# Inverse roots of the latent, query, key and neighbourhood-key norms moved from GpSimd's power to ScalarE's square root and VectorE's reciprocal

## The reference

```python
h = rms_norm(x, g_mix_norm); proj = h @ w_in
q  = (rms_norm(c_q, g_q_a) @ w_q_b).reshape(B, S, 8, 96)
kv = (rms_norm(c_kv, g_kv_a) @ w_kv_b).reshape(B, S, 8, 128)
q_nope = rms_norm(q_nope, g_q[:64]) * scale
q_pe = rope(rms_norm(q_pe, g_q[64:])) * scale
k_nope = rms_norm(k_nope, g_k[:64])
k_pe = rope(rms_norm(k_pe, g_k[64:]))
# dense attention of q on k; then 2-D neighbourhood attention:
q = rms_norm(na_q, g_q) * dh ** -0.5; k = rms_norm(na_k, g_k)
# rms_norm(x, g) = x * rsqrt(mean(x * x) + EPS) * g
x = x + concat(rms_norm(o_A), rms_norm(o_B)) @ w_out
x = x + hier_moe(rms_norm(x))          # top 1 group, top 2 of its 4 experts
```

## Time and profile before

| | us |
|---|---|
| median of 3 runs | 536.64 |
| the three runs | 536.80, 536.64, 532.17 |
| span of the profiled execution | 534.7 |
| TensorE busy in it | 479.6 (90%) |
| GpSimd busy | 171.8 (32%) |
| VectorE busy | 218.4 (41%) |
| ScalarE busy | 146.0 (27%) |
| mean granted TensorE clock | 0.947 of full |

### The profile page before, as it was taken

One profiled execution on the slowest core, in us unless ns is written; L12 is line 12 of the kernel. 1 busy time (PEld: TensorE's weight loads), 2 busy tenths in 40 slices (PEclk: granted clock), 3 DMA queues, 4 the chain that ended last, 5 costly groups with the idle time before them and its releaser, 6 DMA issues. The chain is left out here.

```text
span 534.7 us, 7730 instructions
## 1 busy us (share of the span) xinstructions
PE 479.6 (90%) x2848; PEld 233.6 (44%) x2848; DVE 218.4 (41%) x688; ACT 146.0 (27%) x332; POOL 171.8 (32%) x175
## 2 busy tenths in 40 slices
PE   4899699998999999999999998619999999999970
PEld 3454454544455556555556555514333333333220
DVE  1125454412375555554555838606322222233110
ACT  2200150404455456553443433300000001100010
POOL 1302078878049980000000202210064222222422
PEclk9999799999699999999999989758999999999995
DMA  7999800000600000058000248983989999999512
GB/s 290 428 371 405 318 0 2 1 0 8 248 1 1 1 0 2 1 218 332 0 2 2 58 179 327 371 317 92 353 309 391 394 373 366 377 386 386 127 15 34
DMA packets 29609, 100.05 MB, mean 187 GB/s; under 512 B 5376, under 2 KB 6912, under 8 KB 29184
## 3 DMA queue, kind: packets, MB, share of 16 engines
q1 hardware_dynamic: 21216, 84.04, 40.4%
q0 software_dynamic: 5904, 8.43, 6.7%
q10 hardware_dynamic: 2448, 7.04, 3.5%
HBM read 77.39 MB, written 35.21 MB: 211 GB/s over the span
## 5 line engine op out<-in xcount | busy, mean ns | idle before, releaser
L1296 PE MATMUL bank<-arena 128*128 128x512 f32 (+1 forms) x256 | 112.7, 589 | 5.2 <-DVE arena L877 3.1
L1605 PE MATMUL bank<-arena 128*32 128x512 f32 x832 | 95.5, 600 | 0.1
L599 POOL DMA_INDIRECT out<-arena x25 | 38.7, 1549 | 128.4 <-issue 72.3
L1296 PEld LDWEIGHTS bank<-arena 128*128 128x128 f32 x256 | 48.5, 197 | 53.9 <-issue 47.7
L1271 PEld LDWEIGHTS bank<-arena 128*128 128x128 f32 (+1 forms) x380 | 46.8, 144 | 47.2 <-issue 41.5
L1271 PE MATMUL bank<-arena 128*128 128x128 f32 (+1 forms) x380 | 56.4, 283 | 11.4 <-DMA arena<-in_x 4.7
L1451 PE MATMUL bank<-arena 128*128 128x512 f32 x112 | 55.5, 619 | 0.5 <-issue 0.5
L1605 PEld LDWEIGHTS bank<-arena 128*32 128x32 f32 x832 | 26.3, 111 | 60.0 <-issue 60.0
L1625 PE MATMUL bank<-arena 128*32 128x512 f32 x416 | 48.4, 593 | 0.9 <-DVE arena L1215 0.8
L953 DVE COPY arena<-bank 128x512 f32<-128x512 f32 (+2 forms) x64 | 35.8, 581 | 23.0 <-PE bank L1271 22.9
L833 ACT ACTIVATE arena<-bank 128x256 f32<-128x256 f32 x13 | 5.0, 384 | 136.3 <-PE bank L1605 136.3
(11 more groups left out here) (162 smaller groups left out, 511.4 us busy)
## 6 DMA issues: line engine op xcount, KB each, us to landing
arena<-in_w_gu SPq DMA_DIRECT2D x17, 2048.0 KB, 14.5
arena<-in_w_dn SPq DMA_DIRECT2D x17, 1024.0 KB
slot_rows<-arena SPq DMA_DIRECT2D x1, 11308.0 KB, 38.0
arena<-slot_rows ACTq DMA_DIRECT2D x13, 514.0 KB
arena<-in_w_out SPq DMA_DIRECT2D x2, 2048.0 KB, 8.2
arena<-in_x SPq DMA_DIRECT2D x4, 512.0 KB, 10.7
arena<-in_w_in_k SPq DMA_DIRECT2D x1, 2048.0 KB, 16.0
arena<-in_w_in_q SPq DMA_DIRECT2D x1, 2048.0 KB, 22.0
```

The source lines that it names most:

```text
L599: nc.gpsimd.indirect_dma_start(out=out_rows, out_offset=bass.IndirectOffsetOnAxis(ap=tag_row[:, g, run:run + 1], axis=0), in_=y_sb[g % 3], ...
L1296: last = nc.tensor.matmul(product_bank(i)[:, 0:width], hT[:, k, t * P:(t + 1) * P], w[:, k, :], start=(k == 0), stop=(k == KD - 1))
L1605: last = nc.tensor.matmul(GU[g % 2][BLK * b:BLK * (b + 1), :], xT[g % 2][:, k, BLK * b:BLK * (b + 1)], w_gu[n % RING][:, k, :], start=(k = ...
```

## The change

Six of the seven power instructions on GpSimd are taken out: latent, four of queries and keys, neighbourhood keys. In place of each ScalarE takes the square root of the variance (`deviation`), and VectorE takes the reciprocal of that. The seventh, for neighbourhood queries, stays on GpSimd, as do the roots of x, of the attention outputs and of x1. The semaphore `s_sqrt` ("deviation_ready") goes from ScalarE to VectorE, and `s_nakr` from VectorE to GpSimd for the neighbourhood keys.

```diff
-                inverse_root(("qk", t), flat(rs_qk[:, t]), 3 * H)
             rotate_q(T - 1)
             for w, (name, buf) in enumerate((("nak", nak), ("naq", naq))):
                 for t in range(T):
                     square(3 * T + w * T + t, sq_qk[t % 2][:, 0:NAW], buf[:, t, :], mme_after(product[name, t]))
-                inverse_root((name, 0), flat(rs_na[:, w]), T * H)
+                if w:
+                    pool.wait_ge(s_var, dve_roots.index((name, 0)) + 1)
...
+                if w:
+                    pool.wait_ge(s_root, root["naq", 0] + 1)
+                else:
+                    pool.wait_ge(s_nakr, 1)
...
+            def deviation(key, v):
+                act.wait_ge(s_var, dve_roots.index(key) + 1)
+                nc.scalar.activation(v, v, ACT.Sqrt).then_inc(s_sqrt, 1)
...
             for t in range(T):
                 projection("lat", t, lat, LAT)
+            deviation(("lat", 0), flat(rs_lat))
             for t in range(2):
                 projection("nak", t, nak, NAW)
             for t in range(T):
                 queries_keys(t)
+                if t > 0:
+                    deviation(("qk", t - 1), flat(rs_qk[:, t - 1]))
             for t in range(2, T):
                 projection("nak", t, nak, NAW)
+            deviation(("qk", T - 1), flat(rs_qk[:, T - 1]))
             qk_turned(0)
...
             qk_turned(2)
+            deviation(("nak", 0), flat(rs_na[:, 0]))
             projection("naq", 3, naq, NAW)
             qk_turned(3)
...
-            dve.wait_ge(s_root, root["lat", 0] + 1)
+            dve.wait_ge(s_sqrt, dve_roots.index(("lat", 0)) + 1)
+            link(nc.vector.reciprocal(rs_lat, rs_lat))
...
             def qk_norm(t):
-                dve.wait_ge(s_root, root["qk", t] + 1)
+                dve.wait_ge(s_sqrt, dve_roots.index(("qk", t)) + 1)
+                link(nc.vector.reciprocal(rs_qk[:, t], rs_qk[:, t]))
...
             for t in range(T):
                 na_means(0, t)
+            nak_scales()
```

More of the change, by code:

```diff
@@ L225, in build @@
         s_x1sq, s_h2s, s_lg, s_lgr = sem("x1_squared"), sem("h2_ready"), sem("logits_ready"), sem("logits_read")
-        s_var, s_root = sem("variance_ready"), sem("root_ready")
+        s_var, s_sqrt, s_root = sem("variance_ready"), sem("deviation_ready"), sem("root_ready")
+        s_nakr = sem("nak_scales_ready")
         s_k, s_zeros, s_zero = sem("constants_in"), sem("zeros_ready"), sem("slots_zeroed")
@@ L273, in bank_read @@
             return (s_tpa if act else s_tpe)[p % 2], sum(same)
-        roots = [("x", t) for t in range(T)] + [("lat", 0)] + [("qk", t) for t in range(T)] + [("nak", 0), ("naq", 0)]
+        roots = [("x", t) for t in range(T)] + [("naq", 0)]
         roots += [("oa", t) for t in range(T)] + [(w, t) for t in range(T) for w in ("ob", "x1")]
@@ L465, in link @@
                 pool.wait_ge(c_pool, n[0])
-            def inverse_root(key, v, n):
-                pool.wait_ge(s_var, dve_roots.index(key) + 1)
-                nc.gpsimd.tensor_tensor(v, v, mhalf[:, 0:n], ALU.pow).then_inc(s_root, 1)
             def inverse_root_of(ms, rs):
@@ L490, in square @@
                 nc.gpsimd.tensor_tensor(dst, src, src, ALU.mult).then_inc(s_sqr, 1)
-            def flat(v):
-                return v.rearrange("p a b -> p (a b)")
             def rotate_q(t):
@@ L502, in _ @@
                 square(t, sq[t % 2][:, 0:LAT], lat[:, t, :], mme_after(product["lat", t]))
-            inverse_root(("lat", 0), flat(rs_lat), 3 * T)
             pool.wait_ge(s_rope, 32)
@@ L515, in _ @@
                     square(3 * T + w * T + t, sq_qk[t % 2][:, 0:NAW], buf[:, t, :], mme_after(product[name, t]))
-                inverse_root((name, 0), flat(rs_na[:, w]), T * H)
+                if w:
+                    pool.wait_ge(s_var, dve_roots.index((name, 0)) + 1)
+                    nc.gpsimd.tensor_tensor(rs_na[:, w].rearrange("p a b -> p (a b)"), rs_na[:, w].rearrange("p a b -> p (a b)"),
+                                            mhalf[:, 0:T * H], ALU.pow).then_inc(s_root, 1)
             pool.wait_ge(s_rb, 16 * H)
@@ L542, in _ @@
             for w, (name, buf) in enumerate((("nak", nak), ("naq", naq))):
-                pool.wait_ge(s_root, root[name, 0] + 1)
+                if w:
+                    pool.wait_ge(s_root, root["naq", 0] + 1)
+                else:
+                    pool.wait_ge(s_nakr, 1)
                 for t in range(T):
@@ L673, in queries_keys, with flat @@
                                    src[:, :, NOPE:]).then_inc(s_mme, 1)
+            def flat(v):
+                return v.rearrange("p a b -> p (a b)")
+            def deviation(key, v):
+                act.wait_ge(s_var, dve_roots.index(key) + 1)
+                nc.scalar.activation(v, v, ACT.Sqrt).then_inc(s_sqrt, 1)
             def qk_turned(t):
@@ L917, in na_means, with nak_scales @@
                     nc.vector.tensor_scalar(rs_na[:, w], ms_na[:, w], 1.0 / DH, EPS, ALU.mult, ALU.add).then_inc(s_var, 1)
+            def nak_scales():
+                dve.wait_ge(s_sqrt, dve_roots.index(("nak", 0)) + 1)
+                nc.vector.reciprocal(rs_na[:, 0], rs_na[:, 0]).then_inc(s_nakr, 1)
             def qk_means(t):
```

## The result

| | before | changed |
|---|---|---|
| runs | 4 | 4 |
| median, us | 536.21 (532.17 to 536.80) | 527.26 (526.54 to 528.47) |
| ratio | | 0.9857 [0.9812, 0.9902] |
| span of the profiled execution | 534.7 | 526.6 |
| mean granted clock | 0.947 | 0.957 |

The change makes the kernel 1.4% faster, where 0.5% was predicted, and 527.26 lies under the range's lower end. On another chip the same change gave 0.9895 [0.984, 0.995]: about 5 us, not 9.

A forecast was written before the change was run, and what follows sets the result against it. TensorE, 90% busy, was taken to bound the kernel, with one wait due to a power, at the latents. Terms -1.8 - 1.1 + 0.25 = -2.65 us took 536.64 to 534.0 us; range 529.5 to 537.7.

The forecast's parts named there:

- the chain of 2.41 us: From the latents' variance to VectorE's scaling: 0.6 us in place of 2.41, so 1.8 us gained.
- the pause: TensorE's wait for VectorE to read the first turned latents: from 4.26 us to about 2.5.
- the table loads: ScalarE's loads before the latents' root and the exponentials: both covered, cost nothing; a rival of 6% had them uncovered, 537.7.
- the margin of tile 3's root: Before tile 0's turning: tile 3's variance ready at 90 to 90.5, over 1 us before ScalarE comes at 91.6.
- ScalarE's queue: Square root before tile 0's turned keys and queries: 0.25 us lost; as a rival, TensorE held up, 6%.
- the clock in the pause: Clock still falls around TensorE's wait but is low for less of the first projections: 1.1 us back, ends 0 and 2.8.
- The clock at the scores: At the scores' start the clock was taken to fall; the rival, 12%, had it stay up: up to 5 us, 529.5.
- GpSimd's powers: Seven powers, 29.8 us on GpSimd: worth nothing by themselves, only where TensorE waits for something they hold up.
- root and queue: Latents' root 1.8 us gained, less 0.25 us for the square root in ScalarE's queue before tile 0's turning: 1.55.

The follow-up runs named there:

- rest_only: Changed kernel with the latents' root again a power on GpSimd, the other five roots on ScalarE and VectorE: 528.80 us, ratio 0.9962.
- delay9: Changed kernel with nine small VectorE operations behind the latents' reciprocal, 1.8 us later: 530.13 us, ratio 0.9997.
- before_more12: Kernel before with twelve more one-column memsets on GpSimd ahead of the attention outputs' roots: 531.02 us, ratio 0.9996.
- filled: TensorE's first group of neighbourhood value projections moved from behind the first scores to ahead of them; on the changed kernel 527.36 us, ratio 0.9885.
- the latents' half: Changed kernel with only the latents' root on ScalarE and VectorE, the other roots again powers on GpSimd: 530.16 us, ratio 0.9924.
- the change again: Changed kernel as it is, run again beside the kernel before: 527.92 us, ratio 0.9895.
- before, filled: Kernel before, powers kept, with the first neighbourhood value projections moved ahead of the first scores: 532.27 us, ratio 0.9997.
- the four kernels made later: Kernel before with 3, 7 or 11 small VectorE operations before the latents' scaling, changed kernel with 5 behind the reciprocal: 534.79, 531.34, 532.45, 527.04 us.

## Why the prediction was wrong

**Right, to a few tenths:** the chain of 2.41 us, 0.55 now (predicted 0.6); the pause (1.8 less); the table loads, both covered, 0.85 and 0.8 us ahead of their activations; the margin of tile 3's root (0.64 us, "over 1"). ScalarE's queue cost 0.10 us, not 0.25: I counted the whole instruction, and the next starts 0.11 behind it. The term's lower end of 0.20 was too high too, though in rest_only the same stage is 0.47 us longer. By these steps and the clock's 1.15 us the profiled execution would have gained 2.9 us, 2.65 predicted.

**Right in the number, and in part by luck:** the clock in the pause, 0.48 + 0.67 = 1.15 us back (1.1 predicted, for a low clock that the shorter pause makes shorter). It was low for 3.4 us in place of 6.8, but it is 3.4 us too in rest_only, delay9 and before_more12, whose pause is 5.1 us. Turning and first projections up to nak 2 take 20.9 us before, 19.7 changed, and 19.4, 19.2 and 19.4 in these three. So the kernel before was compared in an execution where the low clock was long; that the shorter pause made it shorter is not shown.

**The step that failed is the sum's silent term that the rest stays as it was**: from the scores to the end it put the gain at nothing, and it took 536.64 as the time from which to subtract. In the profiled execution that rest gained 5.0 us (3.89 - 0.41 + 1.56). Three things are in it.

*The clock at the scores.* I held a fall there for the rule and a clock that stays up for a rival of 12%. It stayed up, and so it did in nearly all the profiles taken since. Of the 19 profiles taken after the one before, one has the fall, and it is one of the changed kernel with six more memsets (0.76 over 131 to 151 us, 23.75 us for the 100 matmuls, in place of 19.86), with the same idle rows of 0.54 and 0.97 us before it as the others that are not filled. So the stretch of waits allows the fall and doesn't decide it. One in 19 makes the fall look too rare for the kernel before: the two profiles that have it are those with the lowest mean clock (0.947 and 0.949; the others have 0.952 to 0.966), and of its 93 runs 38 are at 0.950 or less, against 3 of 17 of the changed kernel. By that, as an estimate, the fall comes in four of ten executions before and in fewer now; that all these runs have it at the scores is not shown. The rival's place was right, its price (up to 5 us) nearly, 3.9; its chance was not.

*One profile and three runs stood for the kernel before.* Over 93 runs in the five sessions it takes 528.1 to 538.3 us, median 532.6: 530.4 where its mean clock is about 0.96 (12 runs), 537.1 where it is about 0.943 (16 runs). At a clock of 0.952 or less were 52 of these 93, and 3 of 17 of the changed kernel. The profiled execution (0.947) and the median of 536.64 are of the slower half. I had seen the one run in three that was 4.5 us faster, and used it for a rival only; it said that the sum was made against one of several levels. Of the 9 us measured at first, some 4 are this choice of runs: the other comparisons give 5.

*The end as TensorE's.* The prediction took the experts to follow TensorE, and put "GpSimd's powers" at "nothing by themselves". There the last to end is GpSimd's chain, which can swallow part of what TensorE gains (in the latents' half the last output comes 10.8 us earlier than before and the end 6.0, with a last lag of 11.4 in place of 6.9), and its start moved with the count of instructions. And the powers of queries and keys were worth about 2 us at the same clock (rest_only 2.1, delay9 2.2, ± 0.7 each), with TensorE's pause as before.

What the gain of about 5 us consists of: 2.7 to 3.6 us at the same clock (the change again, and with six memsets; ± 1.0), where root and queue were to give 1.55; and 0.006 and 0.003 more of mean clock in the same two sets (0.955 against 0.950, 0.956 against 0.953 beside them), 2.3 and 1.1 us by the slope, where 1.1 was predicted. The unfilled halves add up to it (1.3 and 2.1 at the same clock). **Open** stays in what way the roots of queries and keys give their part. GpSimd's gap is the candidate, and its price is resolved only as 1.1 ± 0.8; "rest only" gives 2.1 ± 0.7 unfilled and, filled, no more than "before, filled", though that one has the gap and it has not. Open too is why low clocks are rarer in the changed kernel at places far behind the pause. That they are rarer is shown by the runs (3 of 17 against 52 of 93); that the shorter pause does it is not, for rest_only, with the pause of before, has a mean clock of 0.959 beside 0.955, and the four kernels made later show only that time and lateness don't go in step.

## What to carry to other kernels

Look for the work that ends last in every stage, above all the last one: a chain of DMAs that each wait for the one before may end a kernel in which TensorE is busy nine tenths of the time, and it gives back or swallows what is gained ahead. Before a change of some tenths of a per cent is priced, have the spread of the kernel's own runs and their clock, and compare at the same clock. And where an engine's result is waited for, its place in the reader's queue can be worth as much as its duration: reading before the fourth rotation gave as much as the new roots, and both together more than either.

## What was not expected of the hardware

- GpSimd stood for 4.9 us with no wait that the profile shows, while a packet of an instruction queue came in (5.8 us in the latents' half, between moves at 376.48 and 382.33, with the packet at 380.5). Twelve one-column memsets elsewhere in its program made it vanish.
- A square root of 12 columns on ScalarE takes 0.21 us and so does one of 24; the next activation starts 0.11 us behind its start. VectorE's reciprocal takes 0.23 us for 12 columns and 0.30 for 24. The power on GpSimd took 2.29 for 12 and 4.3 in the mean of the seven.
- The same kernel on one core varies by 1.9% from run to run, and the mean clock accounts for most of it: 4.1 us for 0.01, with 1.0 us left over.
- One execution of the kernel with twelve more memsets took 721.6 us at a mean clock of 0.649; the other 11 took 526.5 to 536.2.
